# Moving the residue of the routed experts' down weights from POOL to DVE in a mixture-of-experts layer

## The chip, the cores and the metric

The kernel runs on one core of a Trainium2 chip. The metric is the device time of one launch in microseconds (us), lower is better. Five engines work side by side on one core and meet only at semaphores: PE (TensorE, matmuls; its weight loads are listed as PEld), DVE (VectorE), ACT (ScalarE), POOL (GpSimd) and SP (SyncE, which here only issues transfers).

## The reference, cut to what matters

The reference is one layer of a streaming encoder: a mixing part (pooling and windowed attention) and then a mixture of experts over 1088 token rows of 1024 numbers. The change lies in the routed experts alone:

```python
N_EXPERTS, TOP_K, D_EXPERT, EXPERT_BLOCK = 64, 6, 256, 128

def swiglu(h, wg, wu, wd):
    return (jax.nn.silu(h @ wg) * (h @ wu)) @ wd

def routed_moe(h, w_router, router_bias, w_gate, w_up, w_down):
    ...                                   # six of 64 experts per row, with weights
    def expert_block(args):               # 128 rows that go to one expert
        xblk, e = args
        return swiglu(xblk, w_gate[e], w_up[e], w_down[e])

    yb = lax.map(expert_block, (xb, block_e))
    y = jnp.zeros((N + 1, D), jnp.float32).at[tok_buf].add(
        yb.reshape(P, D).astype(jnp.float32) * w_buf[:, None])
```

All of it is in float32. An expert's gate, up and down matrices have 1024 x 256, 1024 x 256 and 256 x 1024 numbers, 1 MB each, so the 64 experts are 192 MB that are read once.

## The kernel before

The first 615 us or so hold the mixing part, the router and the shared expert. Then comes a loop over 83 tiles; a tile is up to 128 rows that go to one expert. The 64 experts have one to three tiles each, in order of the expert's number, so a tile is either the first of its expert (call it a new tile) or a further one.

PE gets float32 accuracy out of three faster passes. Each operand is split into a rounded part (hi) and what the rounding left out, the residue (lo), and a product is hi·hi + lo·hi + hi·lo. `passes` writes these as lines 1622, 1623 and 1624. The rounded parts of the weights are made by ACT (gate and up at line 967, down at line 971), the residues by a subtraction raw − hi in `split_rest` (line 477), of 128 x 2048 numbers for each of the three matrices. Before the change DVE makes the residues of gate and up, and POOL that of down. Whichever engine makes it, the row in the trace has line 477; the tile name tells them apart (`hi_gate_up` or `hi_down`).

Four ring slots hold the weights of four experts (`RING`); a residue replaces the raw weights that it was made from. Rounded parts have two slots (`HIS`). SP loads gate and up of an expert four ahead when the slot's last matmul on gate and up is done, and down when the one on down is done.

Each engine runs its own list of instructions in program order, and no scheduler moves anything. In iteration i of the loop:

- PE (`tile`): transposes the activations of tile i−1 (`act_t`, line 1715, the first matmuls of a tile), multiplies gate and up of tile i (24 matmuls), transposes the rows of tile i+1 (line 1704), finds the slots of tile i+3 (line 1697), and multiplies down of tile i−1 (12 matmuls, `expert_out`).
- ACT: rounds down of this tile's expert if the tile is new, applies silu (line 1064), copies the transposed rows (`xTh`, line 1031), rounds gate and up of the next expert if tile i+1 is new, scales and stores the output of tile i−1 (line 1044, `y_of`), and copies the transposed activations (line 1039).
- DVE: silu times up (`act_of`, line 1355), the residue of the rows (`xt_rest`, line 1368), the indices of tile i+3 (`slots`, lines 1344 to 1351), two small columns (`slot_columns`, lines 1377 and 1378), a one-hot matrix (line 1334), and then `rests`: if tile i+1 is new, the residue of the following expert's gate, then in any case the residue of the activations (`at_rest`, line 1373), then that of up.
- POOL: if the tile is new, the residue of down of this tile's expert (`down_rest`), then the gather of the rows of tile i+3 (an indirect DMA, line 781) and the scatter that adds the output of tile i−1 into `y_acc` (line 789). A scatter waits until the one before it has landed.

DVE's `slot_columns` of tile i−1 wait until the scatter of tile i−3 has landed, since they overwrite the columns that it read. PE's `expert_out` waits for the residue of its expert's down weights (`lo_d`).

The flags that say whether a tile is new come from a table in memory. An engine's sequencer loads them with instructions of its own (lines 1400 and 1401 on DVE), and each conditional block has register instructions ahead of the work in it.

Of the kernel before, what the change touches and what calls it, by code (L numbers as in the profile page):

```python
# [51 lines left out]
NE, TOPK, EG, TOPG = 64, 6, 8, 4  # L52
# [28 lines left out]
def build(nc, x_prompt, x_sample, c_prompt, c_sample, state_pool, cache_k, cache_v, w_ada, b_ada,  # L81
# [3 lines left out]
    with ExitStack() as ctx:  # L85
        def sb(name, shape, dt=F32):
            return ctx.enter_context(nc.sbuf_tensor(name, shape, dt))

        def sem(name):
            return ctx.enter_context(nc.semaphore(name))  # L90
# [63 lines left out]
        etab = sb("etab", [1, TAB], I32)  # L154
        ftab = sb("ftab", [1, TAB], I32)
# [118 lines left out]
        def bank(b):  # L274
            return ps[:, b, :]

        def pair(b):
            return ps[:, b:b + 2, :].rearrange("p b n -> p (b n)")
# [96 lines left out]
        round_d = sem("round_d")  # L375
        lo_gu = sem("lo_gu")
        lo_d = sem("lo_d")
# [86 lines left out]
        def raw_of(e, m):  # L464

            return raw[m][:, bass.ds(((e + 1) & (RING - 1)) * WSLOT, MAT)]

        def lo_of(e, m, n=1):
            return lor[:, bass.ds(((e + 1) & (RING - 1)) * WSLOT + m * MAT, n * MAT)]

        def hi_of(e, m, n=1):
            if m == 2:
                return hi_dn[:, bass.ds((e & (HIS - 1)) * WSLOT, MAT)]
            return hi_gu[:, bass.ds((e & (HIS - 1)) * WSLOT + m * MAT, n * MAT)]

        def split_rest(eng, e, m):
            return eng.tensor_tensor(lo_of(e, m), raw_of(e, m), hi_of(e, m).bitcast(F32), ALU.subtract)  # L477
# [189 lines left out]
        def _(pool):  # L667
# [45 lines left out]
            for n, (qc, _, _, _, _) in enumerate(CHUNKS):  # L713
                if n >= 2:
                    pool.wait_ge(sc_mm, n - 1)
                for h in range(2):
                    r = slice(64 * h, 64 * h + 64)

                    pool.tensor_copy(qbd[n % 2][r, :, r], q[r, :, qc:qc + CHUNK]).then_inc(qbd_s, 1)
                    pool.wait_ge(qbd_s, 2 * n + h + 1)  # L720
# [57 lines left out]
            def gather(i, b):  # L778
                pool.wait_ge(idx_s, i + 1)
                pool.sem_inc(pool_turn, 1)  # L780
                pool.indirect_dma_start(out=xg[b], out_offset=None, in_=h2_rows,  # L781
                                        in_offset=bass.IndirectOffsetOnAxis(ap=idxg[b][:, 0:1], axis=0),
                                        bounds_check=gather_bound, oob_is_err=False).then_inc(gathered[b], 16)

            def scatter_add(i, b):
                pool.wait_ge(added, 16 * (i + 2))
                pool.wait_ge(yw_s, i + 2)
                pool.sem_inc(pool_turn, 1)
                pool.indirect_dma_start(out=y_acc, out_offset=bass.IndirectOffsetOnAxis(ap=idxs[b][:, 0:1], axis=0),  # L789
                                        in_=yw[b], in_offset=None, bounds_check=add_bound,  # L790
                                        compute_op=ALU.add).then_inc(added, 16)

            def down_rest(e):

                pool.wait_ge(round_d, e + 1)
                split_rest(pool, e, 2).then_inc(lo_d, 1)

            pool.wait_ge(uz_s, 3)
            gather(0, 0)
            gather(1, 1)  # L800
            pool.wait_ge(xt_mm, 1)
            gather(2, 0)
            down_rest(0)
            pool.wait_ge(xt_mm, 2)
            gather(3, 1)
            for b in range(2):
# [3 lines left out]
            last = pool.value_load(lasti[0:1, NE - 1:NE], min_val=NE - 1, max_val=MAX_TILES - 1)  # L810

            def tile(i, odd):
                f = pool.value_load(ftab[0:1, bass.ds(i, 1)], min_val=0, max_val=2)
                e = pool.value_load(etab[0:1, bass.ds(i, 1)], min_val=0, max_val=NE - 1)
                with pool.If(f > 0):
                    down_rest(e)
                pool.wait_ge(xt_mm, i + 2)
                gather(i + AHEAD, 1 - odd)
                scatter_add(i - 1, 1 - odd)
            tiles(pool, tile, last)  # L820
            last_tile(pool, last, scatter_add)

# [264 lines left out]
        def _(dve):  # L1087
# [64 lines left out]
            for i, (_, kind, gain_row) in enumerate(VECS):  # L1152
                for k in range(KD):
                    m = KD * i + k
                    dve.wait_ge(piece_in[m % PIECES], 16 * (m // PIECES + 1))
                    for c in range(2):
                        if k == 0:
                            dve.tensor_scalar(acc[c], piece[m % PIECES], sil[:, k, c:c + 1], None, ALU.mult).then_inc(acc_s, 1)
                        else:
                            dve.wait_ge(acc_s, 2 * m + c - 1)  # L1160
                            dve.scalar_tensor_tensor(acc[c], piece[m % PIECES], sil[:, k, c:c + 1], acc[c],
                                                     ALU.mult, ALU.add).then_inc(acc_s, 1)

                dve.wait_ge(bg_in, 16 * sum(1 + (g is not None) for _, _, g in VECS[:i + 1]))
                dve.wait_ge(row_mm, i + 1)
                for c in range(2):
                    row = rowsb[:, kind, c, :]
                    link(dve.tensor_tensor(row, pair(6 if c == 0 else 4), brow, ALU.add))
                    if kind == 1:
                        dve.scalar_tensor_tensor(row, row, 1.0, grow, ALU.add, ALU.mult).then_inc(row_s, 1)  # L1170
                    elif gain_row is not None:
                        dve.tensor_tensor(row, row, grow, ALU.mult).then_inc(row_s, 1)
                    else:
                        dve.sem_inc(row_s, 1)
# [155 lines left out]
            def one_hot(i, e=None):  # L1330

                if e is None:
                    e = dve.value_load(etab[0:1, bass.ds(i, 1)], min_val=0, max_val=NE - 1)
                dve.scalar_tensor_tensor(oh, pos[:, bass.ds(e, 1), :].rearrange("p a t -> p t a").to_broadcast([P, NT, P]),  # L1334
                                         base[:, bass.ds(i, 1)], iota1[:, :].unsqueeze(1).to_broadcast([P, NT, P]),
                                         ALU.subtract, ALU.is_equal).then_inc(oh_s, 1)
# [16 lines left out]
            def act_of(i):  # L1353
                dve.wait_ge(silu_s, i + 1)
                dve.tensor_tensor(act_m, sg, bank(4)[:, DE:2 * DE], ALU.mult).then_inc(act_s, 1)

            def mat_rest(e, m):
                dve.wait_ge(round_gu, 2 * e + m + 1)
                split_rest(dve, e, m).then_inc(lo_gu, 1)

            def gate_up_rest(e):

                for m in range(2):
                    mat_rest(e, m)

            def xt_rest(i):
                dve.wait_ge(xt_s, i + 1)
                dve.tensor_tensor(xTl, pair(0).rearrange("p (k n) -> p k n", k=KD), xTh.bitcast(F32), ALU.subtract)\  # L1368
                    .then_inc(xtl_s, 1)

            def at_rest(i):
                dve.wait_ge(at_s, i + 1)
                dve.tensor_tensor(aTl, bank(5)[:, 0:DE].rearrange("p (k n) -> p k n", k=KF), aTh.bitcast(F32), ALU.subtract)\  # L1373
                    .then_inc(atl_s, 1)
# [9 lines left out]
            slots(1, 1, first=True)  # L1384
            gate_up_rest(0)
            xt_rest(0)
            one_hot(2)
            gate_up_rest(1)
            act_of(0)
            xt_rest(1)  # L1390
            slots(2, 0)
            one_hot(3)
# [4 lines left out]
            def rests(i):  # L1397


                f = dve.value_load(ftab[0:1, bass.ds(i + 1, 1)], min_val=0, max_val=2)  # L1400
                e = dve.value_load(etab[0:1, bass.ds(i + 1, 1)], min_val=0, max_val=NE - 1)
                with dve.If(f > 1):
                    mat_rest(e + 1, 0)
                at_rest(i)
                with dve.If(f > 1):
                    mat_rest(e + 1, 1)
            rests(0)

            def tile(i, odd):
# [28 lines left out]
        def _(pe):  # L1438
# [94 lines left out]
            def scores(n):  # L1533
                b, (qc, kc, nk, _, _) = n % 2, CHUNKS[n]
                pe.wait_ge(qbd_s, 2 * (n + 1))
                if n >= 2:
                    pe.wait_ge(ex_s, n - 1)
                for j in range(NJ):
                    ins = pe.matmul(ps[:, 2 * b + j // 2, 192 * (j % 2):192 * (j % 2) + nk], qbd[b][:, j, :],  # L1539
                                    kT[:, kc:kc + nk], start=True, stop=True)  # L1540
                ins.then_inc(sc_mm, 1)
# [236 lines left out]
```

## Time and profile before

| | before |
|---|---|
| time, median of 3 runs | 1586.16 us (1584.53 to 1591.79) |
| span of the profiled execution | 1597.5 us |
| busy over the span: PE, DVE, ACT, POOL | 88%, 69%, 48%, 48% |
| the loop, first tile opened to last tile opened (614.7 to 1543.5 us) | 928.8 us for 82 tiles |
| busy in the loop: PE, DVE, ACT, POOL | 856, 783, 570, 625 us |
| mean busy share of the DMA engines in the loop | 0.89 |

The profile is of one execution. It gives no time for that execution beside its span from the first to the last instruction, and that span is 11.3 us (0.7%) above the median of the three runs; durations below come from it. An engine's busy time says how long its instructions stood in it, also while one of them was held up by something else.

### The profile page before, as it was taken

Reading aid. Unit: us, or ns where it says so; the run is one execution under the profiler, and the core shown is the slowest. Engines: PE = TensorE matmul, PEld = TensorE weight load, DVE = VectorE, ACT = ScalarE, POOL = GpSimd, SP = SyncE. Lnnn points to the kernel's source line nnn. Section 1 sums busy time; section 2 is a strip of 40 time slices with the busy share of each in tenths; the row PEclk is TensorE's granted clock in tenths of the full one; section 3 lists DMA queues with packets and bytes.
Section 4 is the critical chain, followed back from the end, with each engine's and each line's share of the span. In section 5 each row is a group of like instructions: output and inputs, shape, how many; then the busy total and the mean of one; then the engine's idle time right before and its main releaser. Section 6 shows DMA issues by size and latency. Waiting matters only on the chain.

```text
span 1597.5 us, 29813 instructions
## 1 busy us (share of the span) xinstructions
PE 1412.1 (88%) x6692; PEld 1003.4 (63%) x6693; DVE 1099.8 (69%) x1586; ACT 769.5 (48%) x981; POOL 769.0 (48%) x353
## 2 busy tenths in 40 slices
PE   6599998999997987998987799999999999989960
PEld 1346545644545766776766577777777777767750
DVE  0355666732224856989979979789878667897846
ACT  1700004532323343856665466567556456666633
POOL 2000001103244524768766566568677556676663
PEclk9799999999998988999998899999999999999985
DMA  9715423032225126989988789899999878899866
GB/s 331 237 52 167 153 77 110 1 119 96 88 86 198 54 86 235 345 271 358 335 244 284 236 260 326 252 280 350 317 291 306 224 217 268 278 325 292 256 164 226
DMA packets 86457, 351.28 MB, mean 220 GB/s; under 512 B 12643, under 2 KB 14791, under 8 KB 69748
## 3 DMA queue, kind: packets, MB, share of 16 engines
q1 hardware_dynamic: 61432, 279.39, 47.2%
q0 software_dynamic: 24704, 71.27, 20.9%
q8 instruction: 20, 0.33, 0.1%
q10 hardware_dynamic: 284, 0.16, 0.0%
q14 instruction: 17, 0.14, 0.0%
HBM read 307.02 MB, written 62.19 MB: 231 GB/s over the span
## 4 chain that ended last, share of the span: by engine, by line
PE 66%; issue 12%; DVE 10%; DVEq 5%; ACT 3%; DMA 3%; POOL 1%; ACTq 0%; SPq 0%; POOLq 0%
PE ps L1622 12%; PE ps L1623 12%; PE ps L1624 11%; PE ps L1592 8%; PE ps L1505 7%; PE ps L1704 3%; DVE lo_ring L477 3%; PE ps L1460 2%; PE ps L1539 1%; PE ps L1715 1%; DVE arena L1334 1%; DMA arena<-in_w_ada_dram 1%; DVEq L1400 1%; DVE xTl L1368 1%; PE ps L1567 1%
## 5 line engine op out<-in xcount | busy, mean ns | idle before, releaser
L477 DVE TENSOR_TENSOR lo_ring<-raw,hi_gate_up (+1 forms) x128 | 333.8, 2609 | 17.6 <-issue 15.7
L477 POOL TENSOR_TENSOR lo_ring<-raw,hi_down (+1 forms) x64 | 338.2, 5285 | 7.2 <-issue 6.3
L1622 PE MATMUL ps<-hi_gate_up,xTh 128*128 x664 | 276.7, 417 | 7.7 <-DVE xTl L1368 7.4
L1623 PE MATMUL ps<-lo_ring,xTh 128*128 x664 | 273.0, 411 | 0.0
L1624 PE MATMUL ps<-hi_gate_up,xTl 128*128 x664 | 267.0, 402 | 0.0
L967 ACT ACTIVATE hi_gate_up<-raw (+1 forms) x128 | 237.9, 1907 | 54.5 <-issue 53.7
L789 POOL DMA_INDIRECT y_acc<-arena,idxs x83 | 174.1, 2098 | 163.0 <-DMA y_acc<-arena,idxs 112.8
L781 POOL DMA_INDIRECT arena<-h_rows,idxg x86 | 141.9, 1650 | 162.5 <-DVE idxg L1351 153.7
L1044 ACT ACTIVATE arena<-ps,wcol 128x1024 f32<-128x1024 f32 x83 | 92.1, 1109 | 154.4 <-DVE idxs L1378 154.3
L1622 PE MATMUL ps<-hi_down,aTh 128*128 x332 | 140.8, 424 | 22.5 <-DVE aTl L1373 20.8
L1622 PEld LDWEIGHTS ps<-hi_gate_up,xTh 128*128 128x128 f32 x664 | 129.7, 195 | 48.2 <-issue 21.9
L1623 PEld LDWEIGHTS ps<-lo_ring,xTh 128*128 128x128 f32 x664 | 129.6, 195 | 34.9 <-issue 2.6
L1350 DVE SCALAR_TENSOR_TENSOR itab<-sl 128x1 f32 (+1 forms) x86 | 139.0, 1617 | 10.2
L1624 PEld LDWEIGHTS ps<-hi_gate_up,xTl 128*128 128x128 f32 x664 | 129.7, 195 | 25.4
L1505 PE MATMUL ps<-arena 128*128 128x512 f32 (+1 forms) x432 | 143.4, 493 | 0.9 <-DVE arena L1130 0.9
L1623 PE MATMUL ps<-lo_ring,aTh 128*128 x332 | 133.8, 403 | 0.0
L1624 PE MATMUL ps<-hi_down,aTl 128*128 x332 | 133.1, 401 | 0.0
L1334 DVE SCALAR_TENSOR_TENSOR arena<-arena,base,iota 128x1152 bf16<-128x1152 f32 x87 | 130.9, 1505 | 3.0 <-issue 2.3
L1368 DVE TENSOR_TENSOR xTl<-ps,xTh 128x1024 fp32r<-128x1024 f32 x84 | 102.4, 1219 | 43.0 <-ACT xTh L1031 42.6
L971 ACT ACTIVATE hi_down<-raw (+1 forms) x64 | 122.7, 1917 | 18.9 <-issue 17.5
L1592 PE MATMUL ps<-arena 128*128 128x512 f32 (+1 forms) x288 | 125.3, 594 | 0.5 <-ACT arena L916 0.5
L1505 PEld LDWEIGHTS ps<-arena 128*128 128x128 f32 x432 | 72.4, 193 | 72.9 <-issue 72.9
(258 smaller groups left out, 2020.6 us busy)
## 6 DMA issues: line engine op xcount, KB each, us to landing
raw<-in_w_gate_dram SPq DMA_DIRECT2D x64, 1024.0 KB, 6.8
raw<-in_w_up_dram SPq DMA_DIRECT2D x64, 1024.0 KB, 10.3
raw<-in_w_down_dram SPq DMA_DIRECT2D x64, 1024.0 KB, 6.9
arena<-in_w_ada_dram SPq DMA_DIRECT2D x32, 512.0 KB, 6.2
arena<-in_w_ada_dram SPq DMA_DIRECT2D x4, 2048.0 KB, 18.6
arena<-in_x_prompt_dram SPq DMA_DIRECT2D x16, 512.0 KB, 6.4
x_rows<-arena SPq DMA_DIRECT2D x8, 512.0 KB, 2.9
h_rows<-arena SPq DMA_DIRECT2D x8, 512.0 KB, 2.6
```

The costliest lines, as they stand in the source:

```text
L477: return eng.tensor_tensor(lo_of(e, m), raw_of(e, m), hi_of(e, m).bitcast(F32), ALU.subtract)
L781: pool.indirect_dma_start(out=xg[b], out_offset=None, in_=h2_rows, in_offset=bass.IndirectOffsetOnAxis(ap=idxg[b][:, 0:1], axis=0), bounds ...
L789: pool.indirect_dma_start(out=y_acc, out_offset=bass.IndirectOffsetOnAxis(ap=idxs[b][:, 0:1], axis=0), in_=yw[b], in_offset=None, bounds_c ...
L967: act.activation(hi_of(e, m), raw_of(e, m), ACT.Copy).then_inc(round_gu, 1)
L971: act.activation(hi_of(e, 2), raw_of(e, 2), ACT.Copy).then_inc(round_d, 1)
L1334: dve.scalar_tensor_tensor(oh, pos[:, bass.ds(e, 1), :].rearrange("p a t -> p t a").to_broadcast([P, NT, P]), base[:, bass.ds(i, 1)], iota ...
L1350: dve.scalar_tensor_tensor(itab[:, bass.ds(i, 1)], sl[:, 0:1], -1.0, sl[:, 1:2], ALU.add, ALU.add)
L1505: ins = pe.matmul(out[:, 0:n_], w1[:, k, P * c:P * (c + 1)], hT[:, k, a:a + n_], start=(k == 0), stop=(k == KD - 1))
L1592: ins = pe.matmul(bank(2 * (t % 2) + half)[0:ROWS[t], :], hT[:, k, P * t:P * t + ROWS[t]], wo[:, k, 512 * half:512 * half + 512], start=(k ...
L1622: pe.matmul(out, at_h[:, k, :], w_h, start=first, stop=False)
L1623: pe.matmul(out, at_h[:, k, :], w_l, start=False, stop=False)
L1624: return pe.matmul(out, at_l[:, k, :], w_h, start=False, stop=last)
```

## The change

POOL no longer makes the residue of down. DVE makes it at the end of `rests`, behind the residues of gate and up; the flag and the expert are then those of tile i+1, so it is the same residue at nearly the same point of the loop. The residue of expert 0 moves in the same way in the part ahead of the loop, behind the residues of expert 1's gate and up. The wait of PE (`lo_d`) is unchanged, and the wait for ACT's rounding (`round_d`) moves with the residue to DVE.

```diff
@@ -790,17 +790,11 @@
                                         in_=yw[b], in_offset=None, bounds_check=add_bound,
                                         compute_op=ALU.add).then_inc(added, 16)
 
-            def down_rest(e):
-
-                pool.wait_ge(round_d, e + 1)
-                split_rest(pool, e, 2).then_inc(lo_d, 1)
-
             pool.wait_ge(uz_s, 3)
             gather(0, 0)
             gather(1, 1)
             pool.wait_ge(xt_mm, 1)
             gather(2, 0)
-            down_rest(0)
             pool.wait_ge(xt_mm, 2)
             gather(3, 1)
             for b in range(2):
@@ -810,10 +804,6 @@
             last = pool.value_load(lasti[0:1, NE - 1:NE], min_val=NE - 1, max_val=MAX_TILES - 1)
 
             def tile(i, odd):
-                f = pool.value_load(ftab[0:1, bass.ds(i, 1)], min_val=0, max_val=2)
-                e = pool.value_load(etab[0:1, bass.ds(i, 1)], min_val=0, max_val=NE - 1)
-                with pool.If(f > 0):
-                    down_rest(e)
                 pool.wait_ge(xt_mm, i + 2)
                 gather(i + AHEAD, 1 - odd)
                 scatter_add(i - 1, 1 - odd)
@@ -1363,6 +1353,10 @@
                 for m in range(2):
                     mat_rest(e, m)
 
+            def down_rest(e):
+                dve.wait_ge(round_d, e + 1)
+                split_rest(dve, e, 2).then_inc(lo_d, 1)
+
             def xt_rest(i):
                 dve.wait_ge(xt_s, i + 1)
                 dve.tensor_tensor(xTl, pair(0).rearrange("p (k n) -> p k n", k=KD), xTh.bitcast(F32), ALU.subtract)\
@@ -1386,6 +1380,7 @@
             xt_rest(0)
             one_hot(2)
             gate_up_rest(1)
+            down_rest(0)
             act_of(0)
             xt_rest(1)
             slots(2, 0)
@@ -1404,6 +1399,8 @@
                 at_rest(i)
                 with dve.If(f > 1):
                     mat_rest(e + 1, 1)
+                with dve.If(f > 0):
+                    down_rest(e)
             rests(0)
 
             def tile(i, odd):
```

On POOL, the body of one iteration before has the flags, the condition and the residue ahead of the gather and the scatter (`raw_54` and `hi_down` are the raw and rounded down weights):

```order
L814 REGISTER_ALU
L814 TENSOR_LOAD etab
L814 ISA x2
L815 COMPARE_AND_BRANCH
L795 REGISTER_ALU
L477 REGISTER_ALU [waits round_d]
L477 ISA
L477 REGISTER_ALU
L477 ISA
L477 TENSOR_TENSOR lo_ring<-raw_54,hi_down 128x2048
L815 UNCONDITIONAL_BRANCH
L817 REGISTER_ALU
```

After the change the same iteration on POOL is only this:

```order
L779 REGISTER_ALU [waits xt_mm]
L781 DMA arena<-h_rows,idxg 128x1024 [waits idx_s]
L786 ISA
L789 DMA y_acc<-arena,idxs 1216x1024 [waits added,yw_s]
L807 REGISTER_ALU
```

Nothing stands ahead of the gather any more. On DVE, between the residue of up (`raw_53`) and the first work of the next iteration, before:

```order
L477 TENSOR_TENSOR lo_ring<-raw_53,hi_gate_up 128x2048
L1405 UNCONDITIONAL_BRANCH
L1355 TENSOR_TENSOR arena<-arena,ps 128x256 [waits silu_s]
L1368 TENSOR_TENSOR xTl<-ps,xTh 128x1024 [waits xt_s]
```

And after (line 1345 is what was 1355, silu times up, and line 1362 what was 1368, the residue of the rows):

```order
L477 TENSOR_TENSOR lo_ring<-raw_53,hi_gate_up 128x2048
L1400 UNCONDITIONAL_BRANCH
L1402 COMPARE_AND_BRANCH
L1357 REGISTER_ALU
L477 REGISTER_ALU [waits round_d]
L477 ISA
L477 REGISTER_ALU
L477 ISA
L477 TENSOR_TENSOR lo_ring<-raw_54,hi_down 128x2048
L1402 UNCONDITIONAL_BRANCH
L1345 TENSOR_TENSOR arena<-arena,ps 128x256 [waits silu_s]
L1362 TENSOR_TENSOR xTl<-ps,xTh 128x1024 [waits xt_s]
```

The residue of down, and its wait for ACT, stand ahead of silu times up of the next tile.

## Rows read from the trace of the kernel before

**Rows 1.** The page: the span, and TensorE's busy time in it.

```profile
span 1597.5 us, 29813 instructions
...
PE 1412.1 (88%) x6692; PEld 1003.4 (63%) x6693; DVE 1099.8 (69%) x1586; ACT 769.5 (48%) x981; POOL 769.0 (48%) x353
```

**Rows 2.** Windows: us; busy and (instructions) by engine; granted clock, DMA share, GB/s.

```profile
614.70:1543.50 928.80, 856.46 (x4511) 679.89 (x4511) 782.57 (x1029) 569.99 (x515) 624.90 (x229) 0.97 0.89 281
823.70:929.20 105.50, 83.41 (x385) 65.20 (x386) 93.84 (x88) 52.93 (x47) 65.03 (x21) 0.85 0.82 258
```

**Rows 3.** Lines in 614 to 1545 us: group, count; busy us, mean ns; idle before.

```profile
L477 POOL TENSOR_TENSOR lo_ring<-raw,hi_down (+1 forms) x64 | 338.2, 5285 | 7.2 <-issue 6.3
...
L477 DVE TENSOR_TENSOR lo_ring<-raw,hi_gate_up x124 | 324.8, 2619 | 17.6 <-issue 15.7 <-ACT hi_gate_up L967 1.6
...
L1350 DVE SCALAR_TENSOR_TENSOR itab<-sl 128x1 f32 (+1 forms) x83 | 138.6, 1669 | 10.1
...
L1334 DVE SCALAR_TENSOR_TENSOR arena<-arena,base,iota 128x1152 bf16<-128x1152 f32 x83 | 125.2, 1509 | 0.7
```

**Rows 4.** Source L789, the scatters: duration ns min/median/max; DMA to landing.

```profile
L789 POOL DMA_INDIRECT y_acc<-arena,idxs x83: 1563/1589/3695, 631.0 to 1552.7; - x83
...
DMA to landing us min/median/max: 6.1/8.8/12.9
```

**Rows 5.** Timeline of all engines, 1024 to 1030 us: start, us, engine, line, tile.

```profile
1025.16 4.62 POOL L477 TENSOR_TENSOR lo_ring<-raw,hi_down  x1 [0.32 <-issue]
...
1025.18 4.62 DVE L1350 SCALAR_TENSOR_TENSOR itab<-sl 128x1 f32 x1
```

**Rows 6.** Timeline of DVE, 855 to 872 us.

```profile
855.10 0.41 DVE L1355 TENSOR_TENSOR arena<-arena,ps 128x256 f32<-128x256 f32 x1
...
857.14 0.16 DVE L1350 SCALAR_TENSOR_TENSOR itab<-sl 128x1 f32 x1
...
857.67 1.42 DVE L1334 SCALAR_TENSOR_TENSOR arena<-arena,base,iota 128x1152 bf16<-128x1152 f32 x1
859.71 2.29 DVE L477 TENSOR_TENSOR lo_ring<-raw,hi_gate_up  x1 [0.62 <-issue]
861.92 0.42 DVE L1373 TENSOR_TENSOR aTl<-ps,aTh 128x256 fp32r<-128x256 f32 x1
862.25 8.00 DVE L477 TENSOR_TENSOR lo_ring<-raw,hi_gate_up  x1
870.18 0.41 DVE L1355 TENSOR_TENSOR arena<-arena,ps 128x256 f32<-128x256 f32 x1
```

**Rows 7.** Timeline of POOL, 855 to 872 us.

```profile
862.96 5.14 POOL L477 TENSOR_TENSOR lo_ring<-raw,hi_down  x1
```

**Rows 8.** Timeline of DVE, 1080 to 1090 us.

```profile
1082.30 2.50 DVE L1350 SCALAR_TENSOR_TENSOR itab<-sl 128x1 f32 x1
...
1086.25 2.28 DVE L477 TENSOR_TENSOR lo_ring<-raw,hi_gate_up  x1
```

**Rows 9.** Timeline of PE, 749 to 761 us: the transposes that open a tile.

```profile
749.96 0.43 PE L1715 MATMUL ps<-ident,arena 128*128 128x128 f32 x2 [0.96 <-issue]
...
760.01 0.38 PE L1715 MATMUL ps<-ident,arena 128*128 128x128 f32 x2
```

**Rows 10.** Timeline of POOL, 1105 to 1140 us.

```profile
1111.17 2.84 POOL L789 DMA_INDIRECT y_acc<-arena,idxs  x1 [2.41 <-DMA y_acc<-arena,idxs]
...
1123.16 3.23 POOL L789 DMA_INDIRECT y_acc<-arena,idxs  x1 [2.03 <-DMA y_acc<-arena,idxs]
...
1135.44 3.33 POOL L789 DMA_INDIRECT y_acc<-arena,idxs  x1 [1.92 <-DMA y_acc<-arena,idxs]
```

**Rows 11.** Windows, the busiest stretch for DMA.

```profile
1070.60:1147.80 77.20, 71.75 (x379) 56.85 (x378) 75.07 (x86) 51.44 (x47) 60.30 (x20) 0.98 1.01 336
```

**Rows 12.** Timeline of ACT, 855 to 872 us.

```profile
859.21 1.91 ACT L971 ACTIVATE hi_down<-raw  x1
```

**Rows 13.** Timeline of DVE, 594 to 610 us, ahead of the loop.

```profile
605.01 0.42 DVE L1355 TENSOR_TENSOR arena<-arena,ps 128x256 f32<-128x256 f32 x1 [3.40 <-ACT arena L1035]
```

## The prediction

> **What bounds the kernel now.** I read the page first: PE is busy for 88% of the span of 1597.5 us [rows 1], so the loop has to be looked at by itself. The windows show its 82 tiles, from 614.7 to 1543.5 us: 928.8 us, 11.33 us a tile [rows 2]. Then the PE timeline: where nothing holds PE up, a tile takes 760.01 − 749.96 = 10.05 us [rows 9]. So PE alone would need 824 us, and 105 us of the loop are waits for other engines; the change can give back no more than that. To find which engine, I sorted the 82 tiles along the timelines by whether DVE makes residues of gate and up in them (a new tile, 62 of them, 124 instructions in [rows 3]) or not. The 62 stand in 18 unbroken runs of one to eight tiles. The 18 tiles that open a run take 10.49 us in the mean (189 us), the 44 that follow in a run 11.82 us (520 us), the 20 others 10.99 us (220 us). Work on DVE and POOL thus sets the pace in the runs.
>
> The timeline of both engines shows how. DVE's index instruction L1350 has one element per partition and takes 0.16 us when nothing disturbs it [rows 6]. When it starts 0.02 us behind POOL's residue it takes 4.62 us and ends with it [rows 5]. A DVE residue that starts at 862.25 runs for 8.00 us in place of 2.28, around POOL's at 862.96 that itself runs 5.14 us [rows 6, 7, 8]. The lines give the total: L1350 138.6 − 83 x 0.16 = 125 us, the residues of gate and up 324.8 − 124 x 2.28 = 42 us, the one-hot 125.2 − 83 x 1.42 = 7 us, so 174 us in which a DVE instruction only stands [rows 3, 6, 8]. In the worst stretch, 823.7 to 929.2 us, five tiles in a row take 15.08 us each this way, and PE's mean granted clock there is 0.85 in place of the loop's 0.97 [rows 2, 6].
>
> **What the change removes and adds.** It removes 63 POOL instructions of 5.29 us in the loop (the 64th is ahead of it) [rows 3], and with them the standing on DVE. It adds 63 instructions to DVE, each 861.92 − 859.71 = 2.21 us from start to start [rows 6], 139 us in all; a residue issues no transfer. So DVE's busy time should fall by about 174 − 139 = 35 us, although it does more.
>
> The time follows from DVE's cycle in a run, not from the busy sum. From one silu times up to the next, 855.10 to 870.18, the cycle is 15.08 us [rows 6]. Without the standing (8.00 − 2.28 = 5.72) it is 9.36, and with the added 2.21 it is 11.57 us. This contains 0.62 us of idle DVE ahead of the first residue [rows 6], in which its sequencer loads the flags. That is why the standing at L1350 is not all given back. Without it, the step from L1350 to the first residue takes 859.71 − 857.14 = 2.57 us [rows 6]; with a standing of 2.34 us it takes 1086.25 − 1082.30 = 3.95 us [rows 8], only 1.38 more. The other 0.96 hid the sequencer's work, which comes to light again.
>
> So, tile by tile: the 44 that follow in a run go from 11.82 to 11.57 us (509 us). In a tile that opens a run DVE is still ahead. The added residue fills idle time there, and I take 10.3 us, between PE's 10.05 and today's 10.49 (185 us). The 20 others have no added work and lose the standing that spills into them; I take 10.1 us (202 us). The sum is 896 us against 929, a gain of 32.
>
> From that I take 4 off for the scatters. In the busiest stretch each starts as soon as the one before it has landed, 11.99 and 12.28 us apart [rows 10], with the DMA engines at a share of 1.01 [rows 11]. In the short tiles behind a run DVE's columns come only just behind the landing they need, so part of the 18 us that the 20 others could give stays with DMA. The bounds of this term are 0 and 18 us.
>
> The other edits are hidden. The new wait of DVE for ACT's rounding of down: behind it on DVE stand silu times up and the residue of the rows, and PE waits for both. ACT's rounding runs 859.21 to 861.12 [rows 12], and DVE would reach the wait at 862.25 + 2.2 = 864.45, so 3.3 us of cover. With no cover it would cost up to 1.91 us in each of 62 tiles, 118 us. PE's wait for the residue: PE needs it a whole tile later than DVE has made it. Ahead of the loop, DVE idles 3.40 us before its first silu times up [rows 13], which covers 2.21. POOL's gathers come earlier, which nobody waits for. Transfers: in the runs the weights are asked for at about today's pace, so they meet the same load.
>
> The Trainium skill, "SBUF — State Buffer", section "SBUF: two separate sides", says that DVE and GpSimd share a pair of ports as an exclusive lock: an instruction of DVE with two SBUF inputs and one of GpSimd that reads SBUF block each other for the whole instruction. The two ends within 0.02 us [rows 5] agree. Taken alone, that rule gives all 174 us of standing back, which is my first rival below; the step of [rows 6, 8] says otherwise.
>
> **Sum.** 32 − 4 = 28 us off the profiled span: 1597.5 − 28 = 1569.5. The span is 0.7% above the median of the runs, so 1569.5 x 1586.16 / 1597.5 = 1558 us.
>
> **Rivals.**
> First, more comes back: the sequencer gets ahead under the longer block of residues and the cycle in a run is 11.57 − 0.96 = 10.61 us. Then the loop is 44 x 10.61 + 18 x 10.2 + 20 x 10.1 = 852 us, 77 less, and the time 1510. For it: without any idle time DVE's instructions fit in that. Against it: the 0.62 us of idle time stands in each of the 15.08 us tiles, where DVE is as late as it can be [rows 6]. It is what the lock rule of that page of the Trainium skill gives by itself.
>
> Second, slower: the chain of scatters becomes the bound. A scatter that starts while DVE runs a residue takes 2.84 to 3.33 us in place of the least 1.56 [rows 4, 10], and landing takes up to 12.9 us under load [rows 4]. The change raises DVE's time in residues and one-hots from 6.0 to 8.3 us of a cycle (two or three of 2.28 and one of 1.42), so more scatters meet one. Its place is DVE's column copy, which waits for the scatter two tiles back. It decides from the cycle at which the gain is gone: (929 − 185 − 202) / 44 = 12.3 us, just above the longest step of [rows 10]. At 13.0 us the loop takes 959 us, 30 more, and the time is 1616. Against it: today the chain catches up in the other tiles, and POOL's own residue no longer stands between gather and scatter.
> The same section of that page of the Trainium skill has a box on DMAs issued by GpSimd, by which DVE can keep it from writing their descriptors. It speaks for this rival; the 3.33 us of [rows 10] agree.
>
> Third, no change: the wait for ACT's rounding, or DMA behind the runs, costs 0.5 us in each of the 44 following tiles, 22 us, of which 6 us of gain are left: 1580. For it: ACT's order puts the output of a tile ahead of the rounding. Against it: 3.3 us of cover.
>
> **How the numbers follow.** My forecast, 1558 us, has 0.66; the first rival 0.10, the second 0.12, the third 0.12. The forecast's own range is 1542 (no loss to DMA and runs at 11.3 us a tile: 4 + 44 x 0.27 = 16 us better) to 1578 (the full 18 us lost and 11.7 in the runs: 14 + 6 = 20 us worse, rounded). The range to 1522 and 1590 takes in the third rival and parts of the two outer ones; some 0.2 stays out. A measurement of this kernel can tell about 0.5%, 8 us, from no change. Faster by more than that, below 1578: nearly all of the forecast, the first rival and a little of the third, 0.74. Within it: most of the third and the end of the forecast, 0.13. Slower: the second and a bit of the third, 0.13.
>
> **What would show it.** In the changed profile L1350's counterpart should take 0.16 us in every tile, and the residues on DVE 2.28 each, 187 or so in the loop. DVE's busy time in the loop should fall to about 748 us, POOL's by 338. The stretch of 15.08 us tiles should be gone, and with it the clock of 0.85: about 26 of the 32 us come from there and the tile behind it. Tiles that follow in a run should be near 11.57 us from start to start, with 0.6 us of idle DVE ahead of the first residue. I would be wrong if they are near 10.6 or above 12.3, if DVE idles on ACT's rounding ahead of the third residue, or if its column copies wait for scatters by more than some 20 us in all.

## The result, and the profile after

| | before | after |
|---|---|---|
| device time, median of 20 runs each | 1595.11 us (1572.18 to 1621.49) | 1593.88 us (1589.76 to 1596.91) |
| ratio, after to before | | 1.0062 [1.0041, 1.0082] |
| profiled execution: its time | not given | 1590.86 us |
| profiled execution: span | 1597.5 us | 1588.7 us |
| the loop of 82 tiles in it | 928.8 us | 922.4 us |

The prediction was 1558 us, faster, in a range from 1522 to 1590. The measured time is 36 us above it, and outside the range. The two medians are equal within 0.1%. The ratio is a little worse than that, because it sets the runs of the changed kernel against those runs of the kernel before that lie within 1.5% of its fastest. What did change is the spread: 49 us before, 7 us after.

The page of the changed kernel answers to [rows 1]. PE's share of the span has not moved:

```profile
span 1588.7 us, 29157 instructions
...
PE 1398.3 (88%) x6692; PEld 988.0 (62%) x6693; DVE 1076.4 (68%) x1650; ACT 773.1 (49%) x981; POOL 471.3 (30%) x288
```

The windows, as in [rows 2]: start and end, length, busy time and instructions of PE, PEld, DVE, ACT and POOL, granted clock, DMA share, GB/s. The first is the loop, the second the same 105.5 us in which the kernel before had its 15.08 us tiles:

```profile
612.30:1534.70 922.40, 845.25 (x4510) 665.03 (x4510) 757.10 (x1089) 573.20 (x515) 329.52 (x165) 0.99 0.90 283
823.70:929.20 105.50, 95.37 (x505) 74.54 (x503) 93.22 (x127) 71.47 (x62) 40.23 (x19) 0.98 0.96 311
```

The clock of 0.85 is 0.98 here. DVE's busy time in the loop is 757 us, 25 less than before, and POOL's is 295 less.

The groups of lines, as in [rows 3] (line 1340 is what was 1350, line 1324 what was 1334):

```profile
L477 DVE TENSOR_TENSOR lo_ring<-raw,hi_gate_up x124 | 283.8, 2288 | 47.4 <-issue 36.5 <-ACT hi_gate_up L957 10.8
...
L477 DVE TENSOR_TENSOR lo_ring<-raw,hi_down x63 | 144.0, 2286 | 2.0 <-ACT hi_down L961 2.0
...
L1324 DVE SCALAR_TENSOR_TENSOR arena<-arena,base,iota 128x1152 bf16<-128x1152 f32 x83 | 117.8, 1419 | 2.7 <-issue 0.5
...
L1340 DVE SCALAR_TENSOR_TENSOR itab<-sl 128x1 f32 x82 | 13.1, 160 | 10.1
```

The standing is gone: the index instruction takes 0.16 us in the mean, the 187 residues 2.29 us, the one-hot 1.42 us. In exchange DVE idles 36.5 us ahead of residues on nothing but its own sequencer ("issue").

The timeline of DVE over one tile that follows in a run, as in [rows 6] (start, duration, line, tile, idle before):

```profile
884.40 0.41 DVE L1345 TENSOR_TENSOR arena<-arena,ps 128x256 f32<-128x256 f32 x1
...
886.99 1.42 DVE L1324 SCALAR_TENSOR_TENSOR arena<-arena,base,iota 128x1152 bf16<-128x1152 f32 x1
889.13 2.29 DVE L477 TENSOR_TENSOR lo_ring<-raw,hi_gate_up  x1 [0.72 <-issue]
...
891.67 2.33 DVE L477 TENSOR_TENSOR lo_ring<-raw,hi_gate_up  x1
893.93 2.28 DVE L477 TENSOR_TENSOR lo_ring<-raw,hi_down  x1
896.13 0.41 DVE L1345 TENSOR_TENSOR arena<-arena,ps 128x256 f32<-128x256 f32 x1
896.46 1.21 DVE L1362 TENSOR_TENSOR xTl<-ps,xTh 128x1024 fp32r<-128x1024 f32 x1
```

From one silu times up (line 1345) to the next is 896.13 − 884.40 = 11.73 us here, with 0.72 us of idle time ahead of the first residue. All three residues lie between the one-hot and the next silu times up.

PE, as in [rows 9], in the tile behind that run. It opens at 896.59 and has no residue in it:

```profile
896.59 0.44 PE L1712 MATMUL ps<-ident,arena 128*128 128x128 f32 x2 [0.63 <-DVE arena L1345]
897.91 0.50 PE L1619 MATMUL ps<-hi_gate_up,xTh 128*128 x1 [0.89 <-DVE xTl L1362]
...
908.19 0.43 PE L1712 MATMUL ps<-ident,arena 128*128 128x128 f32 x2 [0.48 <-issue]
```

It still takes 908.19 − 896.59 = 11.60 us. Inside it PE waited 0.89 us for the residue of the rows, and 0.48 us ahead of the next opening for nothing that the profile names; there its own sequencer was still loading expert numbers (line 1686). The 0.63 us of waiting for silu times up lie ahead of its opening, so they count in the tile before it. Silu times up and the residue of the rows both stand on DVE behind the residue of down at 893.93.

Waits from 614 to 1560 us: who waits for whom, total us, times, longest:

```profile
DVE lo_ring L477 <- issue: 36.5, 56, 1.6
PE ps L1619 <- DVE xTl L1362: 35.2, 46, 0.9
...
PE ps L1712 <- DVE arena L1345: 28.6, 42, 1.5
...
DVE wcol L1371 <- issue: 5.8, 1, 5.8
...
DVE lo_ring L477 <- ACT hi_down L961: 2.0, 1, 2.0
```

PE waits 64 us for silu times up and the residue of the rows. DVE waits for ACT's rounding of down once, in the last tile of the loop, and its columns are late once, behind the loop.

### The profile page after: what moved, and what is told of

Read it like the earlier page. It is cut to its first block, busy times and chain, and to the rows that moved or that the text cites. A ratio compares the mean times of both kernels' runs of the same rounds, so it can differ in the third digit from the quotient of the medians.

```text
span 1588.7 us, 29157 instructions
## 1 busy us (share of the span) xinstructions
PE 1398.3 (88%) x6692; PEld 988.0 (62%) x6693; DVE 1076.4 (68%) x1650; ACT 773.1 (49%) x981; POOL 471.3 (30%) x288
## 4 chain that ended last, share of the span: by engine, by line
PE 57%; issue 13%; DVE 11%; ACT 8%; DVEq 5%; ACTq 3%; DMA 2%; POOL 1%; POOLq 0%; SPq 0%
PE ps L1619 9%; PE ps L1502 9%; PE ps L1620 8%; PE ps L1621 8%; PE ps L1589 8%; ACT hi_down L961 4%; DVE lo_ring L477 3%; DVE xTl L1362 3%; PE ps L1701 2%; DVEq L1409 2%; PE ps L1457 2%; PE ps L1536 1%; ACT hi_gate_up L957 1%; PE ps L1564 1%; PE ps L1566 1%
## 5 line engine op out<-in xcount | busy, mean ns | idle before, releaser
L477 DVE TENSOR_TENSOR lo_ring<-raw,hi_gate_up (+1 forms) x128 | 292.7, 2288 | 47.4 <-issue 36.5
L1619 PE MATMUL ps<-hi_gate_up,xTh 128*128 x664 | 273.2, 411 | 38.6 <-DVE xTl L1362 37.9
L781 POOL DMA_INDIRECT arena<-h_rows,idxg x86 | 159.7, 1857 | 479.2 <-DVE idxg L1341 446.9
L789 POOL DMA_INDIRECT y_acc<-arena,idxs x83 | 180.5, 2175 | 145.2 <-DMA y_acc<-arena,idxs 79.3
L477 DVE TENSOR_TENSOR lo_ring<-raw,hi_down (+1 forms) x64 | 146.3, 2286 | 2.0 <-ACT hi_down L961 2.0
L1324 DVE SCALAR_TENSOR_TENSOR arena<-arena,base,iota 128x1152 bf16<-128x1152 f32 x87 | 123.4, 1419 | 5.0 <-issue 2.9
L1089 DVE TENSOR_SCALAR ss<-ss 128x1 f32<-128x1 f32 (+3 forms) x25 | 5.4, 218 | 152.6 <-ACT arena L938 71.3
```

The costliest lines, as they stand in the source:

```text
L1619: pe.matmul(out, at_h[:, k, :], w_h, start=first, stop=False)
```

## The experiments

All tile times below are read from the opening transposes on PE in one profiled execution of each kernel, and sorted as in the prediction: 44 tiles that follow in a run, 18 that open one, 20 others, of which 18 stand right behind a run. The column of times has the medians.

| kernel | time us | loop us | follow | open | others | right behind a run |
|---|---|---|---|---|---|---|
| before, as profiled | | 928.8 | 11.82 | 10.49 | 10.99 | 10.98 |
| after | 1593.88 | 922.4 | 11.60 | 10.60 | 11.05 | 11.08 |
| after again | 1593.62 | 925.9 | 11.69 | 10.54 | 11.09 | 11.05 |
| no residue of down | 1538.90 | 860.5 | 10.50 | 10.46 | 10.50 | 10.47 |
| that, and no scatter | 1469.28 | 807.4 | 9.78 | 9.82 | 10.02 | 9.89 |
| after, no scatter | 1579.21 | 914.8 | 11.62 | 10.07 | 11.12 | 11.09 |
| early loads | 1549.75 | 880.3 | 10.77 | 10.30 | 11.05 | 11.04 |
| early loads, down a tile later | 1548.16 | 875.4 | 10.81 | 10.06 | 10.93 | 10.94 |
| before, second execution | 1575.20 | 905.3 | 11.37 | 10.31 | 10.98 | 11.02 |
| before, third execution | 1621.54 | 956.8 | 12.34 | 10.49 | 11.26 | 11.21 |
| before, early loads | 1583.71 | 926.2 | 11.86 | 10.37 | 10.89 | 10.80 |

**The changed kernel again**, unaltered.

> The changed kernel once more, unaltered, on the chip of the next three runs. Theory A (DVE's in-order list sets the pace: each of the 62 new tiles at 11.57 us, the 20 others at PE's 10.1): loop 919 to 925 us, span within 5 us of 1588.7, since nothing in it depends on how two engines happen to meet. Rival C (the missing gain is an accident of the one profiled execution): a loop nearer 896 us and a time near 1565.

Loop 925.9 us, span 1586.7, median 1593.62 us (6 runs). The loop lies 0.9 us above the band of theory A; rival C falls: two executions agree within 4 us of loop. That theory A's sum is near is partly luck. The tiles that open a run take 10.54 us, not 11.57, and the 20 others 11.09, not 10.1: the work that it puts into the first shows up in the second.

**No residue of down.** DVE only signals, and PE takes the rounded weights twice:

```diff
-                split_rest(dve, e, 2).then_inc(lo_d, 1)
+                dve.sem_inc(lo_d, 1)
...
-                swiglu_out(2, aTh, aTl, hi_of(e, 2), lo_of(e, 2)).then_inc(dn_mm, 1)
+                swiglu_out(2, aTh, aTl, hi_of(e, 2), hi_of(e, 2)).then_inc(dn_mm, 1)
```

> Leaves out the residue of the routed down weights: DVE only signals, and PE multiplies the rounded weights once more in its place, so PE's work and all transfers stay. Theory A: DVE's cycle falls from 11.57 by 2.21 to 9.36 us, under PE's 10.05, so nearly all tiles go to 10.1: loop about 830 us, time about 1500. Rival B (the transfers of weights and the chain of scatters set what is left): loop not under 870 us, time not under 1545, with PE waiting for residues that wait for a load or DVE's columns waiting for a scatter.

1538.90 us (1534.15 to 1544.81). The loop, then two of its waits:

```profile
614.50:1474.90 860.40, 822.66 (x4510) 664.10 (x4510) 620.82 (x1026) 566.73 (x515) 315.41 (x163) 1.00 0.93 303
```

```profile
POOL y_acc L789 <- DMA y_acc<-arena,idxs: 400.6, 69, 8.4
...
DVE wcol L1371 <- DMA y_acc<-arena,idxs: 76.8, 39, 5.1
```

Neither theory alone. The loop fell by 62 us, but stopped 30 us short of theory A's 830, and stretches of 11 to 13.7 us tiles are left. In them the scatters set the pace. DVE first, then POOL, at one such place:

```profile
722.23 0.15 DVE L1371 COPY wcol<-wtab 128x1 f32 x1 [2.17 <-DMA y_acc<-arena,idxs]
...
722.52 1.42 DVE L1324 SCALAR_TENSOR_TENSOR arena<-arena,base,iota 128x1152 bf16<-128x1152 f32 x1
```

```profile
722.96 2.44 POOL L789 DMA_INDIRECT y_acc<-arena,idxs  x1 [6.71 <-DMA y_acc<-arena,idxs]
...
735.11 2.43 POOL L789 DMA_INDIRECT y_acc<-arena,idxs  x1 [7.35 <-DMA y_acc<-arena,idxs]
```

DVE's columns wait for a landing, and the next scatter is sent off by the same landing. So the scatter begins while DVE runs the one-hot that follows the columns, and takes 2.44 us in place of the least 1.56 [rows 4]. The columns wait like this 39 times, and 38 of the scatters behind them begin within the one-hot. From scatter to scatter is 12.15 us: DVE has room, but the chain has none.

**That, and no scatter.** From the kernel just shown:

```diff
-                pool.indirect_dma_start(out=y_acc, out_offset=bass.IndirectOffsetOnAxis(ap=idxs[b][:, 0:1], axis=0),
-                                        in_=yw[b], in_offset=None, bounds_check=add_bound,
-                                        compute_op=ALU.add).then_inc(added, 16)
+                pool.dma_start(y_acc[N:N + 64, 0:16], yw[b][0:64, 0:16]).then_inc(added, 16)
```

> The run without the residue of down on DVE, and now also without the scatter that adds the outputs: POOL sends 4 KB to spare rows in its place, so the outputs are never added. Theory B (with room on DVE the chain of scatters, each waiting until the one before has landed, is the floor): the stretches of 11 to 13.7 us tiles go, nearly all tiles take PE's 9.7 to 10.1, loop 800 to 825 us, time about 1490. Rival F (the transfers of the weights are the floor): loop not under 845 us.

1469.28 us (1469.18 to 1472.19). The loop:

```profile
610.10:1417.50 807.40, 803.21 (x4510) 663.15 (x4510) 622.46 (x1026) 566.87 (x515) 197.09 (x165) 1.00 0.74 272
```

Theory B holds for what was left: 807 us, 9.85 us a tile, PE busy for 803 of them (the time is 21 us below the 1490 expected). Rival F falls: the transfers of the weights alone do not bind at this pace.

**The changed kernel without the scatter.** The same edit, made to the changed kernel.

> The changed kernel without the scatter, in the same way. Theory A (DVE's list sets its pace, not the scatters): the tiles that follow in a run stay at 11.5 to 11.7 us, loop 910 to 925 us, time 1580 to 1594. Rival B (scatters hold a good part of it): loop under 900 us.

1579.21 us (1574.85 to 1582.84). The loop:

```profile
610.40:1525.20 914.80, 837.86 (x4511) 664.46 (x4511) 755.49 (x1089) 574.43 (x515) 198.59 (x165) 0.99 0.65 240
```

Theory A holds: 914.8 us, and the tiles that follow take 11.62 us; the time lies 0.8 us below its band. So in the changed kernel the scatters cost 8 us of loop (922.4 − 914.8; 11 by the second execution), and it lies in the tiles that open a run (10.60 to 10.07, 9.5 us in all). Set against the run before it, which differs by the residue of down (and by what PE takes in its place), the residue costs 914.8 − 807.4 = 107 us of loop: 81 in the tiles that follow, 4.6 in those that open a run, and 22 in the others, where no residue stands.

**Early loads.** In the changed kernel DVE's loads of flag and expert numbers go to the head of its tile:

```diff
             def tile(i, odd):
+                f_next, e_next = flags(i)
+                e = dve.value_load(etab[0:1, bass.ds(i + AHEAD + 1, 1)], min_val=0, max_val=NE - 1)
                 act_of(i)
                 xt_rest(i + 1)
-                e = dve.value_load(etab[0:1, bass.ds(i + AHEAD + 1, 1)], min_val=0, max_val=NE - 1)
...
-                rests(i)
+                rests(i, f_next, e_next)
```

> The changed kernel with DVE's loads of the flag and the expert numbers moved to the head of its tile, ahead of silu times up. Theory A: the 0.6 us of idle DVE ahead of the first residue goes in each of 62 new tiles, cycle 10.95 us, 62 x 0.6 = 37 us off: loop about 885, time about 1557. The loads could cost as much at the head, where PE waits for silu times up: then no change. Rival B: under 15 us off, time not under 1579.

1549.75 us (1540.52 to 1551.78), 44 us less than the changed kernel on the same chip; ratio to the kernel before 0.984 [0.979, 0.989]. The loop, and one cycle of DVE:

```profile
611.70:1492.00 880.30, 825.71 (x4510) 659.52 (x4510) 752.81 (x1089) 570.02 (x515) 307.33 (x164) 1.00 0.92 297
```

```profile
899.43 0.41 DVE L1345 TENSOR_TENSOR arena<-arena,ps 128x256 f32<-128x256 f32 x1
...
903.35 2.28 DVE L477 TENSOR_TENSOR lo_ring<-raw,hi_gate_up  x1
...
910.29 0.41 DVE L1345 TENSOR_TENSOR arena<-arena,ps 128x256 f32<-128x256 f32 x1
```

Theory A holds: the idle time ahead of the first residue is gone, and the cycle is 910.29 − 899.43 = 10.86 us where 10.95 was expected. The loads cost nothing at the head: no idle time stands ahead of silu times up in this cycle, so the sequencer had done them while the residues before it were still executing. The 44 us are 7 more than expected, and they are not spread over 62 tiles: against the second execution of the changed kernel the 44 that follow fell by 0.92 us each, those that open a run by 0.24, the others by 0.04.

**Early loads, and the residue of down a tile later.** From the kernel just shown:

```diff
-            def rests(i, f, e):
-                with dve.If(f > 1):
-                    mat_rest(e + 1, 0)
+            def rests(i, f, e, now=None):
+                if now is not None:
+                    with dve.If(now[0] > 0):
+                        down_rest(now[1])
                 at_rest(i)
                 with dve.If(f > 1):
-                    mat_rest(e + 1, 1)
-                with dve.If(f > 0):
-                    down_rest(e)
+                    gate_up_rest(e + 1)
...
+                now = flags(i - 1)
...
-                rests(i, f_next, e_next)
+                rests(i, f_next, e_next, now)
```

The edit does two things more than the expectation names: the residue of gate now stands behind that of the activations, and each tile loads one more flag and expert number.

> As the run before it, and the residue of down is made one tile later, at the head of the residues of the tile that uses it first, ahead of the residue of the activations. Theory A: the opening tile of each of the 18 runs then holds two residues, 8.7 us of DVE's work, and takes PE's 10.1; the third of the run's last expert falls into a tile with idle time: 44 x 10.95 + 38 x 10.1 = 866 us of loop, time about 1538. Rival B: the same time as the run before it within 6 us.

1548.16 us (1545.38 to 1550.44). The loop:

```profile
614.50:1489.90 875.40, 824.69 (x4510) 660.17 (x4510) 750.70 (x1089) 570.22 (x515) 305.55 (x165) 1.00 0.92 299
```

A miss for theory A: 1.6 us off, where 19 were expected; the loop fell by 5. The tiles that open a run did go to 10.06, but the tiles right behind a run stayed at 10.94: the last tile of a run still holds three residues, and PE waits 11.1 us behind the runs for the residue of the rows, as it does in the run before (11.5 us). One stretch of four tiles in which scatters are late (13.3, 12.6, 11.2, 11.8 us) took back 6 us. It is the fastest kernel that computes everything, by less than the two medians can be told apart.

**Two more executions of the kernel before**, unaltered.

> The kernel before once more, one execution with a profile, to see from which base the gain was to be counted. Theory D (how often DVE and POOL block each other differs from one execution to the next, and with it the time): the sum of standing on DVE, 174 us in the execution that the prediction read, and the number of tiles over 13 us (12 there) differ by a third or more from that, and the loop moves with them, between 900 and 945 us. Rival E (the standing is the same each time, and something else varies): standing within 165 to 183 us.

> As the run before it: a further execution of the kernel before. Theory D: again another sum of standing and another loop; of the executions seen, the longer loop has the more tiles over 13 us. Rival E: as above.

They took 1575.20 and 1621.54 us, nearly the two ends of its range. The loop and the groups of the first:

```profile
614.00:1519.30 905.30, 836.56 (x4511) 665.96 (x4511) 783.29 (x1029) 569.24 (x515) 620.99 (x228) 0.99 0.90 289
```

```profile
L477 DVE TENSOR_TENSOR lo_ring<-raw,hi_gate_up x124 | 289.1, 2331 | 14.9 <-issue 12.8 <-ACT hi_gate_up L967 2.1
...
L1350 DVE SCALAR_TENSOR_TENSOR itab<-sl 128x1 f32 (+1 forms) x83 | 187.5, 2259 | 10.1
...
L1334 DVE SCALAR_TENSOR_TENSOR arena<-arena,base,iota 128x1152 bf16<-128x1152 f32 x83 | 116.8, 1407 | 0.4
```

And of the second:

```profile
609.10:1565.90 956.80, 868.54 (x4510) 689.22 (x4510) 808.66 (x1029) 570.18 (x515) 620.13 (x229) 0.95 0.87 273
```

```profile
L477 DVE TENSOR_TENSOR lo_ring<-raw,hi_gate_up x124 | 353.1, 2848 | 19.7 <-issue 17.1 <-ACT hi_gate_up L967 2.1
...
L1334 DVE SCALAR_TENSOR_TENSOR arena<-arena,base,iota 128x1152 bf16<-128x1152 f32 x83 | 134.1, 1616 | 0.7
...
L1350 DVE SCALAR_TENSOR_TENSOR itab<-sl 128x1 f32 (+1 forms) x83 | 126.1, 1519 | 10.1
```

With the terms of the prediction, the standing is 174 + 6 + 0 = 180 us in the first (index, residues, one-hot) and 113 + 70 + 16 = 199 us in the second, against 125 + 42 + 7 = 174 in the execution that the prediction read. So theory D is wrong on the sum, which differs by 14% at most (rival E's band holds the first but not the second), and right that the loop moves: 905, 929 and 957 us, the last beyond its band. What goes with the loop is the part that stands at the residues: 6, 42 and 70 us. The tiles over 13 us, of which the expectation counted 12 in the execution that the prediction read, are 14 there by the opening transposes, and 5 and 19 in these two. The same run of tiles in the two executions, first the quick one, then the slow one:

```profile
721.68 0.41 DVE L1355 TENSOR_TENSOR arena<-arena,ps 128x256 f32<-128x256 f32 x1
...
723.72 2.48 DVE L1350 SCALAR_TENSOR_TENSOR itab<-sl 128x1 f32 x1
...
730.18 2.28 DVE L477 TENSOR_TENSOR lo_ring<-raw,hi_gate_up  x1
732.38 0.41 DVE L1355 TENSOR_TENSOR arena<-arena,ps 128x256 f32<-128x256 f32 x1
```

```profile
737.12 0.41 DVE L1355 TENSOR_TENSOR arena<-arena,ps 128x256 f32<-128x256 f32 x1
...
744.30 8.00 DVE L477 TENSOR_TENSOR lo_ring<-raw,hi_gate_up  x1
752.23 0.41 DVE L1355 TENSOR_TENSOR arena<-arena,ps 128x256 f32<-128x256 f32 x1
```

The quick one goes round in 10.70 us and stands at the index instruction; the slow one goes round in 15.11 us and stands at the residue of up, for 8.00 us. There are 0, 6 and 12 tiles over 14.5 us in the executions with loops of 905, 929 and 957 us. Six more such tiles, each 15.11 − 10.70 = 4.4 us longer, make 26 us; the loops lie 24 and 28 us apart.

POOL's residue of down in the same two cycles, again the quick one first:

```profile
730.88 6.06 POOL L477 TENSOR_TENSOR lo_ring<-raw,hi_down  x1
```

```profile
745.00 5.14 POOL L477 TENSOR_TENSOR lo_ring<-raw,hi_down  x1
```

In both DVE's residue of up starts 0.70 us ahead of POOL's (730.18 and 744.30). In the quick one it goes through in 2.28 us and POOL's takes longer; in the slow one it is held until POOL's has ended. In the execution that the prediction read this meeting ends the first way 12 times and the second way 6 times, in these two 14 and 0, and 6 and 10 times. So which of the two starts first in the trace doesn't decide it.

**Early loads in the kernel before.** The edit of the early loads, made to the kernel before.

> The kernel before (residue of down on POOL) with DVE's loads of the flag and the expert numbers at the head of its tile. It tells whether the gain of the early loads belongs to the changed kernel. Theory G (the loads cost only where DVE's list sets the pace: in the kernel before that is in the tiles of 15.1 us, 0 to 12 of an execution): 0.6 x 12 = 7 us off at most, median between 1575 and 1605. Rival H (they cost 0.6 us in each of the 62 new tiles in either kernel): 37 us off, median under 1565.

1583.71 us (1575.77 to 1595.91, 12 runs) beside 1598.75 (1572.23 to 1626.92, 17 runs); ratio, taken as above, 1.000 [0.997, 1.003]. Rival H falls: the median is not under 1565. The median lies in theory G's band, but its 7 us are not shown: the quickest executions are alike, while 10 of the 17 without the edit are longer than the longest of the 12 with it, and the medians lie 15 us apart. Whether the early loads make the slow pattern rarer was not followed up. The loop of the profiled execution, which is the longest of the 12, is 926 us, and the residues stand 320.1 − 124 x 2.28 = 37 us:

```profile
L477 DVE TENSOR_TENSOR lo_ring<-raw,hi_gate_up x124 | 320.1, 2581 | 5.9 <-issue 5.1 <-ACT hi_gate_up L967 0.7
```

## Why the prediction was wrong

**What was right.** The added and the removed work came out as worked out: residues of 2.29 us, no standing, the 15.08 us tiles and the low clock gone. The cycle in a run was to be 11.57 us and is 11.60 in the mean over 44 tiles (510.5 us for 509). The idle time ahead of the first residue, against which the first rival was weighed, is there with 0.72 us, and the early loads show that it was real: without it the cycle is 10.86. Both covers held (2.0 us of waiting for ACT in all; PE never waits for the residue of down). The second rival was to decide from a cycle of 12.3 us, and the cycle stayed below; its mechanism is real, though, since it is what holds the kernel without the residue at 860 us. DVE's busy time was to be 748 and is 757. POOL's fell by 295 in place of 338; 24 us of the difference are gathers and scatters, which take longer now.

**The step that failed.** "The 20 others have no added work and lose the standing that spills into them; I take 10.1 us". They take 11.05 us: 221 us in place of 202. Most of the excess lies in the 18 of them that stand right behind a run, and two things were wrong there.

First, the added residue is paid in them. DVE goes through its list in order, and all residues of a new tile stand ahead of the silu times up and the residue of the rows on which the next tile's start depends. So DVE's lag at the end of a run reaches into the tile behind it: PE waits there for the residue of the rows in 12 of the 18 tiles, 9.2 us in all. The two kernels without scatters show it cleanly: with the residue of down on DVE the 18 tiles take 11.09 us, and PE waits 14.6 us in 17 of them; without it they take 9.89. The tile that opens a run does hide its residue, as I had said (10.07 us without scatters). I counted that slack there, and then again in the tile behind.

Second, nothing showed that DVE's standing held these tiles before. They took 10.98 us, and I had put all of the excess down to the blocking between DVE and POOL. But PE waits in them for DVE only once, 0.6 us, in the kernel before; 10.5 us are waits at an opening for which the profile names no engine, and 7.0 us of that kind are left after the change (3.1 of them at the end of the last tile, in both kernels). So the waits for DVE make up about half of the 18 us above 10.1 us a tile; what makes the rest is open.

The tiles that open a run were mis-sized too: 10.60 for 10.3, 5.8 us in all. There it was the scatters, which I had put at 4 us and which measure 8 to 11.

**The base.** The second error is not in the loop. I took the time as 1586.16/1597.5 of the span, on the ground that the profiled execution was 0.7% above the median of the runs. But its span is longer than each of the three times of that median, so it was an execution of its own; with the 2 us of the next sentence it lies some 4 us above the median of 20. The time of an execution lies about 2 us above its span: 1590.86 and 1588.7 for the changed kernel, 1575.20 and 1573.5 for the kernel before.

The 36 us then come out as: 1.5 in the tiles that follow, 5.8 in those that open a run, 19.1 in the others, less the 4 set aside for scatters and 0.8 of rounding: 21.6 us in the loop; −2.4 us outside it; 13.7 us from scaling the span by 0.993 in place of adding 2.2; 3.0 us between the profiled execution and the median of its kernel. The sum is 35.9.

**Where the expected gain went.** The page of the Trainium skill that the prediction named ("SBUF — State Buffer", "SBUF: two separate sides") has DVE and GpSimd block each other, and three executions agree, with 174, 180 and 199 us of standing. So engines do not meet at semaphores alone, as I had written ahead of the prediction. But a total of standing isn't a price. Where a standing falls on DVE's early instructions it costs little, and the kernel before goes round in 10.70 us; where it falls on the last residue of a tile, the cycle is 15.11. The tiles that follow in a run thus take 11.37, 11.82 or 12.34 us in the mean of an execution before, and 11.60 or 11.69 after. Against the quick executions the change loses, against the slow ones it wins, and in the median it is the same. This is shown for the three executions that have a trace. What decides into which of the two a run of tiles falls is open: the same meeting of two residues, 0.70 us apart, ends either way.

## What to carry to other kernels

Where one engine's in-order list sets the pace, count the tiles that wait for it, not the tiles in which its work stands: its lag at the end of a run is paid in the next tile, and slack may be counted only once. Where a term says that a wait goes away, name the row that shows the wait. Before taking a profile as the base of a sum, look at the spread of the times; where two engines block each other, profile the kernel several times and see which pattern the one at hand is in. And when a stall that covered a sequencer's loads is taken away, move the loads in the same edit to where a long instruction still covers them: that was worth 44 us here, the change by itself nothing.

## What the runs showed that I had not expected

The kernel before goes through the same instructions in 10.70 or in 15.11 us a tile, and changes between the two within one execution; its time ranges over 3%, and in the three traced executions it rises with the number of slow tiles. In the execution with 12 slow tiles PE's mean granted clock over the loop is 0.95, in the one with none it is 0.99.

Scatters can lock themselves to DVE: where DVE's columns wait for a landing, the next scatter begins within DVE's one-hot, 38 times of 39, and takes 2.44 us in place of 1.56.
